# GLA scores in a fused transformer kernel: the diagonal moves from a level of its own into the finest level's matmuls

## The chip, the cores and the metric

The kernel runs on one core of a Trainium2 chip. A core has TensorE (matmuls, from SBUF into PSUM; PE in the profile, its weight loads PEld), VectorE (DVE), ScalarE (ACT), GpSimd (POOL) and SyncE (SP, which issues the weight transfers here). The engines run side by side and wait for each other by semaphores. The metric is device time in microseconds of one execution of the whole program.

## The reference, cut to what matters

Two transformer blocks over 256 tokens of width 1024. The change touches only gated linear attention (GLA) in the second layer of the second block: 4 heads, keys of 128, values of 256, chunks of 64 tokens.

```python
def _gla_chunked(q, k, v, log_a):
    gc = jnp.cumsum(chunks(log_a), axis=3)
    def step(state, inp):
        qi, ki, vi, gi = inp
        g_end = gi[:, :, -1, :]
        o_inter = jnp.einsum('bhtd,bhdv->bhtv', qi * jnp.exp(gi), state)
        rel = gi[:, :, :, None, :] - gi[:, :, None, :, :]
        decay = jnp.exp(jnp.where(causal[:, :, None], rel, -jnp.inf))
        scores = jnp.einsum('bhtd,bhsd,bhtsd->bhts', qi, ki, decay)
        o_intra = jnp.einsum('bhts,bhsv->bhtv', scores, vi)
        state = jnp.exp(g_end)[..., None] * state + jnp.einsum(
            'bhsd,bhsv->bhdv', ki * jnp.exp(g_end[:, :, None, :] - gi), vi)
        return state, o_inter + o_intra
```

What has to come out is, for each head, a causal matrix of scores between queries t and keys s, each the sum over 128 key channels of q * k * exp(g_t - g_s), with g the running sum of log decays; then scores times values.

## The kernel before

**Layout.** Features lie on the 128 partitions and the 256 tokens along the free axis, in two tiles t of 128 tokens. `gla` holds 24 rows of 256: queries of the four heads are `gla[:, 0:4]`, keys `gla[:, 4:8]`, gates from 16 on. `D[0]` to `D[3]` are PSUM banks of 512 fp32 columns.

**Scores by levels.** exp(g_t - g_s) is split at a token m between s and t, into exp(g_t - g_m) on the query and exp(g_m - g_s) on the key. `LEVELS = (64, 32, 16, 8, 4, 2, 1)`: at level n the tokens fall into blocks of 2n, the right half of each block are queries, the left half keys, and m is the last token of the left half. So each pair s < t of one tile belongs to exactly one level, and the pairs s = t need no decay: they are level 0, the plain product of keys and queries, of which only the diagonal is kept. At level 1 (the seventh and finest) m is the key's own token, so keys are multiplied by exp(0). Scores between tile 0 and tile 1 come from an eighth pass, `scores_across`.

**Who does what, for level index i:**
- VectorE, `exponents(i)`: the differences of `gla_g` (running sums) into `gla_e` or `gla_z` by turns, in two instructions of 512 elements, one for each half.
- ScalarE, `decays(i)`: exp of all 1024 elements in place.
- VectorE, `decayed(i)`: keys and queries times these, in two instructions of 512 elements, into `gla_w[i % 2]`; then `level_ready`.
- TensorE, `gla_level(i)`: for each tile, four matmuls (one a head) of 128 keys against 64 queries, into a bank; level 0 has 128 queries.
- VectorE, `keep_level(i)`: for each tile one conditional copy from the bank into `gla_s` through `level_mask`, then `drained_dve`.

VectorE goes through `exponents(i + 1)`, `decayed(i)`, `keep_level(i - 1)` in the loop over i, and evicts weight chunks in between. The last `keep_level` and a copy of the scores across end in `gla_scores_done`, for which the output matmuls (`d<-gla_s,gla_v`) wait.

**Weight chunks.** All projections stream fp32 weights in chunks of 128 x 2048. ScalarE rounds a chunk to `w_hi` (L1121), VectorE subtracts for `w_lo` (L1625), and TensorE multiplies in three products (fp32r), waiting for `lo_done` at the start of each chunk. Chunks 4 to 7 of `gla_in` are the values, with 512 columns a matmul. TensorE takes these in the order chunk 4, level 0, chunk 5, level 1, chunk 6, levels 2 and 3, chunk 7, levels 4 and 5, chunk 8, levels 6 and 7, chunk 9 with `scores_across` in it at k = 6, then the output matmuls, their sums of squares, chunks 10 and 11, and the output projection. VectorE writes `w_lo` of chunk 5 right behind `decayed(1)` and ahead of `keep_level(0)`.

**Order.** Everything is written out by hand: each engine executes its own list in the order of the code, and a PSUM bank is taken with `acquire` once its last reader has counted up.

The lines of the profile: L592 every matmul, L1619 products (`mul`), L1625 subtractions (`sub`), L1622 additions, L1629 `fused`, L2353 the conditional copy in `keep_level`, L2392 the copy of the scores across, L1121 every ScalarE function.

Of the kernel before, what the change touches and what calls it, by code (L numbers as in the profile page):

```python
# [30 lines left out]
P = 128  # L31
T = 256
# [144 lines left out]
def program(nc, io, out):  # L177
    with ExitStack() as stack:
        place = {"at": (nc.sbuf_base + 31) // 32 * 32}

        def at(name, offset, shape, dtype=F32):
            return nc.alloc_sbuf_tensor_at(name, [P] + shape, dtype, offset=offset)
# [246 lines left out]
        def over(ap, n):  # L429

            return ap.unsqueeze(1).broadcast_to([P, n, ap.shape[-1]])
# [5 lines left out]
        def flat(ap):  # L437
            return ap.rearrange("p a t -> p (a t)")
# [16 lines left out]
        def right_halves(ap, n):  # L455

            return ap.rearrange("p (b x t) -> p b x t", x=2, t=n)[:, :, 1, :]
# [115 lines left out]
        def _(pe):  # L573
# [17 lines left out]
            def mm(out, lhsT, rhs, start=True, stop=True):  # L591
                return pe.matmul(out, lhsT, rhs, start=start, stop=stop, skip_group_check=True)  # L592
# [469 lines left out]

            def gla_level(i):

                if i == 0:
                    pe.wait_ge(evicted, FIRST_OUT["gla_in"] + 4)
                else:
                    pe.wait_ge(level_ready, count.next(level_ready))
                for t in range(TT):
                    b = (2 * i + t) % 4  # L1070
                    cols = slice(t * P, (t + 1) * P)
                    acquire(b)
                    for h in range(4):
                        if i == 0:
                            last = mm(D[b][:, h * P:(h + 1) * P], gla[:, 4 + h, cols], gla[:, h, cols])
                        else:
                            k = gla_w[i % 2][:, h, cols]
                            last = mm(D[b][:, h * P // 2:(h + 1) * P // 2], k, right_halves(k, LEVELS[i - 1]))
# [37 lines left out]
        def _(act):  # L1116
# [3 lines left out]
            def fn(out, in_, func=ACT.Copy, **kw):  # L1120
                return act.activation(out, in_, func, **kw)  # L1121
# [493 lines left out]
        def _(dve):  # L1615
            count = Counts(dve)

            def mul(out, a, b):
                return dve.tensor_tensor(out, a, b, ALU.mult)  # L1619
# [525 lines left out]
            def conv_ffn(layer, ple_moving):  # L2145
# [117 lines left out]
                def half_finish(f):  # L2263

                    dve.wait_ge(act_done, count.next(act_done))
                    m, tile = ple_mul[:, 1, f, :], x[:, 6 + f, :]
                    mul(m, ple_sig[:, 1, f, :], D[3][:, f * T:(f + 1) * T]).then_inc(drained_dve, count.one(drained_dve))
                    dve.wait_ge(drained_dve, count.sent[drained_dve])
                    add(tile, tile, m).then_inc(x_gated, count.one(x_gated))

                half_evict(0)
# [16 lines left out]

            def gla_evict(j, split=True):
                if j < 2:  # L2290
                    fused(gla[:, 2 * j:2 * j + 2, :], bank_of("gla_in", j, j % U), float(P) ** -0.5, over(rstd[:], 2),
                                    ALU.mult, ALU.mult).then_inc(evicted, count.one(evicted))
# [39 lines left out]
            def decayed(i):  # L2332

                e = (gla_e, gla_z)[i % 2]
                dve.wait_ge(expo_done, count.next(expo_done))
                level = LEVELS[i - 1] if i <= len(LEVELS) else P
                to, ev = blocks(gla_w[i % 2], level), blocks(e, level)
                q, k = (flat(gla[:, f:f + 4, :]).rearrange("p (b h t) -> p b h t", h=2, t=level) for f in (0, 4))
                mul(to[:, :, 0, :], k[:, :, 0, :], ev[:, :, 0, :]).then_inc(dve_own, count.one(dve_own))
                mul(to[:, :, 1, :], q[:, :, 1, :], ev[:, :, 1, :]).then_inc(level_ready, count.one(level_ready))  # L2340

            def keep_level(i):

                dve.wait_ge(drained_dve, count.sent[drained_dve])
                for t in range(TT):
                    dve.wait_ge(full_dve, count.next(full_dve))
                    to, keep, found = gla_s[:, t, :, :], over(level_mask[:, i, :], 4), as_tiles(D[(2 * i + t) % 4][:], P)
                    if i > 0:
                        n = LEVELS[i - 1]
                        to = to.rearrange("p h (b x t) -> p h b x t", x=2, t=n)[:, :, :, 1, :]  # L2350
                        keep = right_halves(level_mask[:, i, :], n).unsqueeze(1).broadcast_to([P, 4, P // (2 * n), n])
                        found = D[(2 * i + t) % 4][:, 0:2 * P].rearrange("p (h b t) -> p h b t", h=4, t=n)
                    dve.copy_predicated(to, keep, found).then_inc(drained_dve, count.one(drained_dve))  # L2353

            ahead("gla_in", 0, 0)
            token_norm()
# [19 lines left out]
            for i in range(1, len(LEVELS) + 1):  # L2376
                if i > 1:
                    dve.wait_ge(level_ready, count.sent[level_ready])
                if i < len(LEVELS):
                    exponents(i + 1)  # L2380
                decayed(i)
                if i == len(LEVELS):
                    exponents(i + 1)
                if i == 1:
                    ahead("gla_in", 3, 0)
                keep_level(i - 1)
                if i in evictions:
                    gla_evict(evictions[i])
            decayed(len(LEVELS) + 1)
# [180 lines left out]
```

## Time and profile before

| | us |
|---|---|
| median of 3 runs | 1025.76 (1025.67 to 1025.93) |
| profiled execution | 1025.8, its span 1023.9 |
| TensorE busy (matmul / weight load) | 1016.1 / 989.9 |
| VectorE busy | 805.7 |
| ScalarE busy | 642.9 |
| mean granted clock of TensorE | 0.999 of 2.4 GHz |

The span is what lies between the first and the last instruction; the rest of the execution's time lies around it. The profile shows an fp32 matmul as two passes, each with a weight load of its own. A pass in the records lasts from its issue to the end of its drain, some 0.28 us for 128 columns, while the next one starts earlier; so what a pass costs is read from the distance of starts, not from its duration.

### The profile page before, as it was taken

To read this page: it belongs to the slowest core of one execution; us is meant where nothing else is said; L and a number is where in the kernel's file an instruction comes from. 1 tells how busy PE (TensorE), PEld (TensorE's weight loads), DVE (VectorE), ACT (ScalarE), POOL (GpSimd) and SP (SyncE) were. 2 spreads that over 40 slices of the span, in tenths; PEclk is the share of its full clock that TensorE was granted. 3 is DMA by queue.
4 is the path that set the end of the run, shared out by engine and by line. 5 is a ranking of instruction groups with operands and counts; after the bars stand their busy time and mean duration, and the time that the engine had idled before them with its cause. 6 is when DMAs were issued, how large, how long until landed. Compare 5 with 4: busy or idle time off the path is not lost.

```text
span 1023.9 us, 21104 instructions
## 1 busy us (share of the span) xinstructions
PE 1016.1 (99%) x8522; PEld 989.9 (97%) x8522; DVE 805.7 (79%) x960; ACT 642.9 (63%) x866; POOL 3.0 (0%) x9
## 2 busy tenths in 40 slices
PE   8999999999999999999999999999999999999998
PEld 7888999899999999999999999999899999999998
DVE  6879976586666756999887777798998888777787
ACT  7666665566455347676785756676546678657573
POOL 0000000000000000000000000010000000000000
PEclk9999999999999999999999999999999999999999
DMA  9942463355555564634655555564433565555541
GB/s 345 279 171 83 165 229 143 124 194 189 192 181 201 199 218 160 196 133 171 220 198 186 213 194 180 173 218 149 157 109 121 180 233 205 183 198 202 192 152 68
DMA packets 30543, 186.99 MB, mean 183 GB/s; under 512 B 3730, under 2 KB 6515, under 8 KB 8852
## 3 DMA queue, kind: packets, MB, share of 16 engines
q1 hardware_dynamic: 29908, 185.09, 51.6%
q8 instruction: 45, 0.74, 0.3%
q10 hardware_dynamic: 576, 1.05, 0.3%
q14 instruction: 14, 0.11, 0.0%
HBM read 183.99 MB, written 1.34 MB: 181 GB/s over the span
## 4 chain that ended last, share of the span: by engine, by line
PE 95%; DVE 3%; DMA 1%; ACT 0%; issue 0%; SPq 0%; DVEq 0%
PE g L592 62%; PE d L592 32%; DVE w_lo L1625 1%; PE d L595 1%; DMA raw<-weights 1%; DVE gla_w L1619 0%; DVE gla_o L1619 0%; DVE go_both L1629 0%; PE g L595 0%; DVE gla_s L2353 0%; DVE ho_both L1625 0%; DVE newton L1619 0%; DVE newton L1629 0%; ACT ho_both L1121 0%; DVE gla_v L1763 0%
## 5 line engine op out<-in xcount | busy, mean ns | idle before, releaser
L1625 DVE TENSOR_TENSOR w_lo<-raw,w_hi 128x2048 fp32r<-128x2048 f32 (+1 forms) x175 | 389.0, 2226 | 88.6 <-ACT w_hi L1121 88.3
L1121 ACT ACTIVATE w_hi<-raw 128x2048 fp32r<-128x2048 f32 (+1 forms) x174 | 326.2, 1878 | 142.4 <-PE g L592 84.4
L592 PE MATMUL g<-f_both,w_hi 128*128 128x256 f32 x1408 | 240.8, 275 | 0.0
L592 PEld LDWEIGHTS g<-f_both,w_hi 128*128 128x128 f32 x1408 | 212.0, 188 | 0.1
L592 PE MATMUL g<-f_both,w_lo 128*128 128x256 f32 x704 | 193.6, 275 | 0.0
L592 PE MATMUL d<-hid_lo,w_hi 128*128 (+1 forms) x528 | 145.2, 275 | 0.0
L592 PE MATMUL d<-hid_hi,w_lo 128*128 (+1 forms) x528 | 145.2, 275 | 0.0
L592 PE MATMUL d<-hid_hi,w_hi 128*128 (+1 forms) x528 | 145.2, 275 | 0.0
L592 PEld LDWEIGHTS g<-f_both,w_lo 128*128 128x128 f32 x704 | 132.2, 188 | 0.0
L592 PE MATMUL g<-x_both,w_hi 128*128 128x256 f32 x704 | 120.0, 275 | 0.0
L592 PEld LDWEIGHTS g<-x_both,w_hi 128*128 128x128 f32 x704 | 106.0, 188 | 0.1
L592 PEld LDWEIGHTS d<-hid_hi,w_hi 128*128 128x128 f32 x528 | 99.1, 188 | 0.0
L592 PEld LDWEIGHTS d<-hid_lo,w_hi 128*128 128x128 f32 x528 | 99.1, 188 | 0.0
L592 PEld LDWEIGHTS d<-hid_hi,w_lo 128*128 128x128 f32 x528 | 99.1, 188 | 0.0
L592 PE MATMUL g<-x_both,w_lo 128*128 128x256 f32 x352 | 96.8, 275 | 0.0
L592 PEld LDWEIGHTS g<-x_both,w_lo 128*128 128x128 f32 x352 | 66.1, 188 | 0.0
L592 PE MATMUL g<-hy_both,w_hi 128*128 128x256 f32 x288 | 50.4, 279 | 0.0
L1121 ACT ACTIVATE conv_out<-conv_in,par 128x256 f32<-128x256 f32 x88 | 47.5, 588 | 1.0 <-DVE conv_in L1619 1.0
L592 PE MATMUL g<-in_both,w_hi 128*128 128x256 f32 x256 | 45.1, 279 | 1.6 <-DVE w_lo L1625 1.6
L592 PE MATMUL g<-gla_both,w_hi 128*128 128x256 f32 x256 | 45.3, 280 | 0.0
L592 PE MATMUL g<-p_both,w_hi 128*128 128x256 f32 x256 | 44.2, 277 | 0.0
L592 PEld LDWEIGHTS g<-hy_both,w_hi 128*128 128x128 f32 x288 | 43.6, 188 | 0.6 <-DVE w_lo L1625 0.3
(363 smaller groups left out, 1964.0 us busy)
## 6 DMA issues: line engine op xcount, KB each, us to landing
raw<-weights SPq DMA_DIRECT2D x168, 1024.0 KB, 4.8
bias_tab<-bias_dram SPq DMA_DIRECT2D x8, 192.0 KB, 7.4
x<-x_t ACTq DMA_DIRECT2D x4, 256.0 KB, 5.5
raw<-weights SPq DMA_DIRECT2D x4, 256.0 KB, 6.6
raw<-weights SPq DMA_DIRECT2D x2, 512.0 KB, 7.4
mem_t<-mem_t SPq DMA_DIRECT2D x1, 1024.0 KB, 9.3
out<-x SPq DMA_DIRECT2D x3, 256.0 KB, 2.2
hy_swap<-hy_qk SPq DMA_DIRECT2D x4, 128.0 KB, 6.0
```

Source lines behind the costliest of these rows:

```text
L592: return pe.matmul(out, lhsT, rhs, start=start, stop=stop, skip_group_check=True)
L595: return pe.transpose(out, src, ident[0:n, 0:n])
L1121: return act.activation(out, in_, func, **kw)
L1625: return dve.tensor_tensor(out, a, b, ALU.subtract)
```

## The change

The diagonal no longer has a matmul of its own. The queries are evicted into a new tile `gla_q`, for each head and tile a row of 192 = 128 queries as they are and 64 places for the finest level's decayed queries. At the finest level the keys need no decay, so only `exponents` and `decayed` for the queries are left (one instruction each, instead of two), ScalarE's exp takes 512 elements instead of 1024, and TensorE multiplies the plain keys with the row of 192. Two heads then fill a bank with 384 columns, so the level takes four banks instead of two. `keep_level` of that level makes, for each tile and pair of heads, two conditional copies: the diagonal of 2 x 128, then the finest scores of 2 x 64, and the second waits for the first since both write `gla_s`. All other levels read the queries from `gla_q`. One increment of a semaphore in the gate of the embedding moves from `drained_dve` to `dve_own`.

```diff
+        gla_q = at("gla_q", TR, [4, TT, 3 * P // 2])
+        FINEST = 3 * P // 2
+        def finest_bank(t, pair):
+            return (2 * len(LEVELS) + 2 * t + pair) % 4
...
             def gla_level(i):
-                if i == 0:
-                    pe.wait_ge(evicted, FIRST_OUT["gla_in"] + 4)
-                else:
-                    pe.wait_ge(level_ready, count.next(level_ready))
+                pe.wait_ge(level_ready, count.next(level_ready))
                 for t in range(TT):
+                    cols = slice(t * P, (t + 1) * P)
+                    if i == len(LEVELS):
+                        for pair in range(2):
+                            b = finest_bank(t, pair)
+                            acquire(b)
+                            for f in range(2):
+                                h = 2 * pair + f
+                                last = mm(D[b][:, f * FINEST:(f + 1) * FINEST], gla[:, 4 + h, cols], gla_q[:, h, t, :])
+                            fill(b, last, full_dve, drained_dve)
+                        continue
...
             gla_chunk(4)
-            gla_level(0)
             gla_chunk(5)
...
+                if i == len(LEVELS):
+                    e = e[:, 1::2]
                 fn(e, e, ACT.Exp, scale=1.0 / 16.0).then_inc(expo_done, 1)
...
+                    if level == 1:
+                        sub(to[:, :, 1, :], s[:, :, 1, :], middle).then_inc(decay_done, 1)
+                        return
...
+                if i == len(LEVELS):
+                    to = gla_q[:, :, :, P:FINEST].rearrange("p h t c -> p (h t) c")
+                    mul(to, queries[:, :, :, 0], factors[:, :, :, 0]).then_inc(level_ready, count.one(level_ready))
+                    return
...
+                    for pair in range(2):
+                        dve.wait_ge(full_dve, count.next(full_dve))
+                        to = gla_s[:, t, 2 * pair:2 * pair + 2, :]
+                        found = D[finest_bank(t, pair)][:, 0:2 * FINEST].rearrange("p (h c) -> p h c", h=2)
+                        dve.copy_predicated(to, over(level_mask[:, 0, :], 2), found[:, :, 0:P]).then_inc(dve_own, count.one(dve_own))
+                        dve.wait_ge(dve_own, count.sent[dve_own])
+                        dve.copy_predicated(right_of(to), keep.broadcast_to([P, 2, P // 2, 1]), found[:, :, P:FINEST].unsqueeze(3)).then_inc(drained_dve, count.one(drained_dve))
...
-                keep_level(i - 1)
+                if i > 1:
+                    keep_level(i - 1)
```

TensorE at the border of chunk 4 and chunk 5 (`d<-gla` is level 0), before:

```order
L592 MATMUL g<-w_hi,gla_both 128x512
L592 MATMUL d<-gla 128x128 [waits lr_ready,evicted]
L592 MATMUL d<-gla 128x128 x3
L592 MATMUL d<-gla 128x128 [waits drained_dve]
L592 MATMUL d<-gla 128x128 x3
L592 MATMUL g<-w_hi,gla_both 128x512 [waits lo_done]
```

and now (lines are 7 further down in the new file):

```order
L599 MATMUL g<-w_lo,gla_both 128x512
L599 MATMUL g<-w_hi,gla_both 128x512
L599 MATMUL g<-w_hi,gla_both 128x512 [waits lo_done]
L599 MATMUL g<-w_lo,gla_both 128x512
L599 MATMUL g<-w_hi,gla_both 128x512 x2
```

The last matmul of chunk 4 is followed directly by the first of chunk 5, which waits for its low weights.

VectorE behind the decayed tiles of level index 1 (`gla_w_167`), before:

```order
L1619 TENSOR_TENSOR gla_w_167<-gla,gla_z 128x8x64 [waits expo_done]
L1619 TENSOR_TENSOR gla_w_167<-gla,gla_z 128x8x64
L1625 TENSOR_TENSOR w_lo<-raw,w_hi 128x2048 [waits hi_done]
L2353 COPY_PREDICATED gla_s<-level_mask,d 128x512 [waits full_dve,drained_dve]
L2353 COPY_PREDICATED gla_s<-level_mask,d 128x512 [waits full_dve]
L1625 TENSOR_TENSOR w_lo<-raw,w_hi 128x2048 [waits hi_done]
L1625 TENSOR_TENSOR gla_z<-gla_g 128x32x16 [waits level_ready]
```

and now:

```order
L1630 TENSOR_TENSOR gla_w_167<-gla,gla_z 128x8x64 [waits expo_done]
L1630 TENSOR_TENSOR gla_w_167<-gla_q,gla_z 128x8x64
L1636 TENSOR_TENSOR w_lo<-raw,w_hi 128x2048 [waits hi_done] x2
L1636 TENSOR_TENSOR gla_z<-gla_g 128x32x16 [waits level_ready]
L1636 TENSOR_TENSOR gla_z<-gla_g 128x32x16
```

Chunk 5's subtraction stands where it stood; the two conditional copies behind it are gone and chunk 6's subtraction has moved up to it.

VectorE at the end of the levels, from the products for the scores across (`gla_w_166`), before:

```order
L1619 TENSOR_TENSOR gla_w_166<-gla,gla_e 128x4x128 [waits expo_done]
L1619 TENSOR_TENSOR gla_w_166<-gla,gla_e 128x4x128
L2353 COPY_PREDICATED gla_s<-level_mask,d 128x256 [waits full_dve,drained_dve]
L2353 COPY_PREDICATED gla_s<-level_mask,d 128x256 [waits full_dve]
L2392 COPY gla_s<-d 128x512 [waits full_dve]
```

and now:

```order
L1630 TENSOR_TENSOR gla_w_166<-gla,gla_e 128x4x128 [waits expo_done]
L1630 TENSOR_TENSOR gla_w_166<-gla_q,gla_e 128x4x128
L2391 COPY_PREDICATED gla_s<-level_mask,d 128x256 [waits full_dve,drained_dve]
L2393 COPY_PREDICATED gla_s<-level_mask,d 128x128 [waits dve_own]
L2391 COPY_PREDICATED gla_s<-level_mask,d 128x256 [waits full_dve]
L2393 COPY_PREDICATED gla_s<-level_mask,d 128x128 [waits dve_own]
...
L2433 COPY gla_s<-d 128x512 [waits full_dve]
```

The pair of conditional copies stands there four times in the new order, ahead of the same copy of the scores across.

## Rows read from the trace of the kernel before

**Rows 1.** The page's first part: busy us, share of the span, instructions.

```profile
PE 1016.1 (99%) x8522; PEld 989.9 (97%) x8522; DVE 805.7 (79%) x960; ACT 642.9 (63%) x866; POOL 3.0 (0%) x9
```

**Rows 2.** Timeline of weight loads that waited: start, us, instruction, [idle before <-releaser].

```profile
728.07 0.19 PEld L592 LDWEIGHTS g<-w_hi,gla_both 128*128 128x128 f32 x1 [0.23 <-DVE w_lo L1625]
...
767.24 0.97 PEld L592 LDWEIGHTS d<-gla_w 128*128 128x128 f32 x8 [0.31 <-DVE gla_w L1619]
777.65 0.73 PEld L592 LDWEIGHTS d<-gla_w,const 128*128 128x128 f32 x4 [0.28 <-ACT gla_w L1121]
...
793.89 0.30 PEld L592 LDWEIGHTS d<-go_both,w_hi 128*128 128x128 f32 x2 [0.33 <-DVE go_both L1629]
```

**Rows 3.** The same view: level 0, its weight loads and its matmuls.

```profile
725.86 1.98 PEld L592 LDWEIGHTS d<-gla 128*128 128x128 f32 x16
...
726.09 1.95 PE L592 MATMUL d<-gla 128*128 128x128 f32 x16
```

**Rows 4.** Timeline of VectorE around chunk 5's low weights and the first merges.

```profile
714.99 0.69 DVE L1619 TENSOR_TENSOR gla<-g,rstd 128x512 f32<-128x512 f32 x1 [0.96 <-PE g L592]
...
725.73 2.28 DVE L1625 TENSOR_TENSOR w_lo<-raw,w_hi 128x2048 fp32r<-128x2048 f32 x1
727.93 1.34 DVE L2353 COPY_PREDICATED gla_s<-level_mask,d 128x512 f32<-128x512 uint8 x2
...
734.80 0.45 DVE L2353 COPY_PREDICATED gla_s<-level_mask,d 128x256 f32<-128x256 uint8 x1 [0.95 <-PE d L592]
```

**Rows 5.** Timeline of weight loads: levels 6 and 7, and chunk 9 behind them.

```profile
759.16 3.66 PEld L592 LDWEIGHTS d<-gla_w 128*128 128x128 f32 x32
762.74 0.30 PEld L592 LDWEIGHTS g<-gla_both,w_hi 128*128 128x128 f32 x2
```

**Rows 6.** Timeline of matmuls: plain fp32 with 256 columns, in two runs of 8 passes.

```profile
775.02 1.89 PE L592 MATMUL d<-sq,const 128*128 128x256 f32 x8
776.75 2.04 PE L592 MATMUL d<-gla_w,const 128*128 128x256 f32 x8
```

**Rows 7.** Timeline of VectorE from the exponents of level 7 to chunk 9's eviction.

```profile
756.01 1.29 DVE L1625 TENSOR_TENSOR gla_z<-gla_g 128x512 f32<-128x512 f32 x2
757.21 1.29 DVE L1619 TENSOR_TENSOR gla_w<-gla,gla_e 128x512 f32<-128x512 f32 x2
...
759.08 1.28 DVE L1619 TENSOR_TENSOR gla_w<-gla,gla_z 128x512 f32<-128x512 f32 x2
760.28 0.75 DVE L1625 TENSOR_TENSOR gla_e<-gla_g 128x256 f32<-128x256 f32 x2
...
765.90 1.28 DVE L1619 TENSOR_TENSOR gla_w<-gla,gla_e 128x512 f32<-128x512 f32 x2
767.11 1.29 DVE L2353 COPY_PREDICATED gla_s<-level_mask,d 128x256 f32<-128x256 uint8 x2
768.44 0.69 DVE L2392 COPY gla_s<-d 128x512 f32<-128x512 f32 x1
769.86 0.69 DVE L1619 TENSOR_TENSOR gla<-g,rstd 128x512 f32<-128x512 f32 x1 [0.73 <-PE g L592]
```

**Rows 8.** Timeline of weight loads: rest of chunk 9, then the output matmuls.

```profile
768.13 0.30 PEld L592 LDWEIGHTS g<-gla_both,w_hi 128*128 128x128 f32 x2
...
769.55 0.30 PEld L592 LDWEIGHTS d<-gla_s,gla_v 128*128 128x128 f32 x2
```

**Rows 9.** Timeline of VectorE: an instruction that reads the result of the one ahead.

```profile
779.62 0.69 DVE L1629 SCALAR_TENSOR_TENSOR newton<-mean_sq,rough 128x512 f32<-128x512 f32 x1
780.35 0.69 DVE L1619 TENSOR_TENSOR newton<-newton,rough 128x512 f32<-128x512 f32 x1
```

**Rows 10.** A stretch by engine (PEclk is the granted clock), and its longest wait.

```profile
5.00:10.00 5.00, 3.40 (x22) 2.75 (x22) 3.92 (x9) 4.19 (x10) 0.00 (x0) 1.00 1.02 368
...
7.13 0.30 PEld L592 LDWEIGHTS g<-in_both,w_hi 128*128 128x128 f32 x2 [1.62 <-DVE w_lo L1625]
```

More of the change, by code:

```diff
@@ L1063, in gla_level @@
             def gla_level(i):
-                if i == 0:
-                    pe.wait_ge(evicted, FIRST_OUT["gla_in"] + 4)
-                else:
-                    pe.wait_ge(level_ready, count.next(level_ready))
+                pe.wait_ge(level_ready, count.next(level_ready))
                 for t in range(TT):
+                    cols = slice(t * P, (t + 1) * P)
[8 more added lines that the diff above has]
+                        continue
                     b = (2 * i + t) % 4
-                    cols = slice(t * P, (t + 1) * P)
                     acquire(b)
                     for h in range(4):
[L1074 to L1078, printed above, removed]
+                        k = gla_w[i % 2][:, h, cols]
+                        last = mm(D[b][:, h * P // 2:(h + 1) * P // 2], k, right_halves(k, LEVELS[i - 1]))
                     fill(b, last, full_dve, drained_dve)
             gla_chunk(4)
-            gla_level(0)
             gla_chunk(5)
@@ L2266, in half_finish @@
                     m, tile = ple_mul[:, 1, f, :], x[:, 6 + f, :]
-                    mul(m, ple_sig[:, 1, f, :], D[3][:, f * T:(f + 1) * T]).then_inc(drained_dve, count.one(drained_dve))
-                    dve.wait_ge(drained_dve, count.sent[drained_dve])
+                    own = (dve_own, drained_dve)[f]
+                    mul(m, ple_sig[:, 1, f, :], D[3][:, f * T:(f + 1) * T]).then_inc(own, count.one(own))
+                    dve.wait_ge(own, count.sent[own])
                     add(tile, tile, m).then_inc(x_gated, count.one(x_gated))
@@ L2290, in gla_evict @@
                 if j < 2:
-                    fused(gla[:, 2 * j:2 * j + 2, :], bank_of("gla_in", j, j % U), float(P) ** -0.5, over(rstd[:], 2),
-                                    ALU.mult, ALU.mult).then_inc(evicted, count.one(evicted))
+                    bank = bank_of("gla_in", j, j % U).rearrange("p f (t c) -> p f t c", c=P)
+                    scale = rstd[:].rearrange("p (t c) -> p t c", c=P).unsqueeze(1).broadcast_to([P, 2, TT, P])
+                    fused(gla_q[:, 2 * j:2 * j + 2, :, 0:P], bank, float(P) ** -0.5, scale, ALU.mult, ALU.mult).then_inc(evicted, count.one(evicted))
                     if j == 1:
@@ L2335, in decayed @@
                 dve.wait_ge(expo_done, count.next(expo_done))
-                level = LEVELS[i - 1] if i <= len(LEVELS) else P
-                to, ev = blocks(gla_w[i % 2], level), blocks(e, level)
-                q, k = (flat(gla[:, f:f + 4, :]).rearrange("p (b h t) -> p b h t", h=2, t=level) for f in (0, 4))
+                if i > len(LEVELS):
+                    mul(gla_w[0][:, :, 0:P], gla[:, 4:8, 0:P], e[:, :, 0:P]).then_inc(dve_own, count.one(dve_own))
+                    mul(gla_w[0][:, :, P:2 * P], gla_q[:, :, 1, 0:P], e[:, :, P:2 * P]).then_inc(level_ready, count.one(level_ready))
+                    return
@@ new lines, in decayed, with in_tiles @@
+                level = LEVELS[i - 1]
+                def in_tiles(ap):
+                    return ap.rearrange("p a (b x n) -> p a b x n", x=2, n=level)
+                queries = in_tiles(gla_q[:, :, :, 0:P].rearrange("p h t c -> p (h t) c"))[:, :, :, 1, :]
+                factors = in_tiles(flat(e).rearrange("p (a c) -> p a c", c=P))[:, :, :, 1, :]
+                if i == len(LEVELS):
+                    to = gla_q[:, :, :, P:FINEST].rearrange("p h t c -> p (h t) c")
+                    mul(to, queries[:, :, :, 0], factors[:, :, :, 0]).then_inc(level_ready, count.one(level_ready))
+                    return
@@ L2339, in decayed @@
+                to, ev, k = blocks(gla_w[i % 2], level), blocks(e, level), blocks(gla[:, 4:8, :], level)
+                right = in_tiles(flat(gla_w[i % 2]).rearrange("p (a c) -> p a c", c=P))[:, :, :, 1, :]
                 mul(to[:, :, 0, :], k[:, :, 0, :], ev[:, :, 0, :]).then_inc(dve_own, count.one(dve_own))
-                mul(to[:, :, 1, :], q[:, :, 1, :], ev[:, :, 1, :]).then_inc(level_ready, count.one(level_ready))
+                mul(right, queries, factors).then_inc(level_ready, count.one(level_ready))
@@ L2342, in keep_level, with right_of @@
             def keep_level(i):
                 dve.wait_ge(drained_dve, count.sent[drained_dve])
+                n = LEVELS[i - 1]
+                keep = right_halves(level_mask[:, i, :], n).unsqueeze(1)
+                def right_of(scores):
+                    return scores.rearrange("p h (b x t) -> p h b x t", x=2, t=n)[:, :, :, 1, :]
                 for t in range(TT):
-                    dve.wait_ge(full_dve, count.next(full_dve))
-                    to, keep, found = gla_s[:, t, :, :], over(level_mask[:, i, :], 4), as_tiles(D[(2 * i + t) % 4][:], P)
@@ L2348, in keep_level @@
[L2348 to L2351, printed above, removed]
-                        found = D[(2 * i + t) % 4][:, 0:2 * P].rearrange("p (h b t) -> p h b t", h=4, t=n)
-                    dve.copy_predicated(to, keep, found).then_inc(drained_dve, count.one(drained_dve))
+                    if i < len(LEVELS):
+                        dve.wait_ge(full_dve, count.next(full_dve))
+                        found = D[(2 * i + t) % 4][:, 0:2 * P].rearrange("p (h b t) -> p h b t", h=4, t=n)
+                        dve.copy_predicated(right_of(gla_s[:, t, :, :]), keep.broadcast_to([P, 4, P // (2 * n), n]), found).then_inc(drained_dve, count.one(drained_dve))
+                        continue
@@ new lines, in keep_level @@
+                    for pair in range(2):
+                        dve.wait_ge(full_dve, count.next(full_dve))
+                        to = gla_s[:, t, 2 * pair:2 * pair + 2, :]
[3 more added lines that the diff above has]
+                        dve.copy_predicated(right_of(to), keep.broadcast_to([P, 2, P // 2, 1]), found[:, :, P:FINEST].unsqueeze(3)).then_inc(drained_dve, count.one(drained_dve))
```

## The prediction

> **What bounds the kernel now.** I read the busy shares of the page first, then every wait of TensorE's weight loads over the whole span, then the stretch from 724 to 794 us engine by engine, because only there the change moves anything. The page says that TensorE is busy for all but about 8 us of the span [rows 1]; so an edit counts by what it does to the row of TensorE's instructions, and time that another engine wins counts only where TensorE waits for it. From the GLA levels to the end such waits are four: 0.23 us for the low part of chunk 5's weights, 0.31 us for the decayed tiles of the scores across chunks, 0.28 us for a square of ScalarE and 0.33 us at the output projection [rows 2]. VectorE is nearly full in the same stretch, so it is the second engine to follow; ScalarE waits for VectorE there.
>
> **Level 0 goes.** Its 8 matmuls are 16 passes (each fp32 matmul shows as two). Their weight loads begin at 725.86 [rows 3] and the next weight load, chunk 5's first, stands at 728.07 with 0.23 idle before it [rows 2]. So they take 2.21 - 0.23 = 1.98 us of TensorE, and I ask what comes next in the row: chunk 5, which waits for the whole low part of its weights. VectorE writes that part from 725.73 to 728.01 [rows 4], and TensorE starts 0.06 later. Nothing ahead of that subtraction on VectorE is removed: the diff takes away only the merge of level 0, which stands behind it. So TensorE arrives 1.98 us earlier and waits 2.2 us instead of 0.23. Gained: **0**. The two evictions of the queries now write pieces of 128 in rows of 192; their element count is the same, and I cost that at nothing: VectorE waits 0.96 us for TensorE a little later, at 714.99, which hides any slowness below that [rows 4].
>
> **VectorE without the merge of level 0.** Two conditional copies of 512 elements, 1.34 us [rows 4], go. The two subtractions behind them move forward, and then VectorE meets the merge of level 1, for which it already waits 0.95 us [rows 4]. That wait grows to about 2.2 us and the merge starts where it did. Gained: 0. The earlier low part of chunk 6 also lets SyncE issue one weight transfer 1.2 us earlier; nobody waits for it.
>
> **Level 7 on TensorE.** Before, levels 6 and 7 are 32 passes of 64 columns from 759.16 to 762.74, 0.112 us each [rows 5]. A pass of 128 columns is no dearer: 16 of them cover 1.95 us with the last one's 0.28 in it, again 0.11 [rows 3]. A pass of 256 columns in plain fp32 takes (776.75 - 775.02) / 8 = 0.216 us [rows 6], twice that of 128. So moving data is what a wide pass costs, and the smaller value is a floor. No fp32 pass of 192 columns with full weights is in the trace: the bounds are the floor, 0.112, and the pass of 256, 0.216. I take the latter by its columns, 0.216 x 192 / 256 = 0.162, since above the floor time should go with columns. 16 passes then cost 16 x 0.050 = **+0.80 us** (bounds 0 and +1.66). Banks do not hold it up: the four banks are those of levels 5 and 6, and VectorE's merge of level 6 ends, as worked out below, earlier than now.
>
> Here the Trainium skill says otherwise ("TensorE: Matmul & The Clock Gate", Back-to-back issue gap and LDWEIGHTS): a warm matmul streams one column per cycle, N / 2.4 + 2.5 ns, and a load of 128 weights takes 128 / 1.2. By that 192 columns would take 82 ns, hide under a load of 107 ns, and level 7 would cost nothing more. The trace disagrees for plain fp32 with its 0.216 us for 256 columns, which is two cycles a column, so I go by the row.
>
> **The wait of 0.31 us ahead of the scores across.** VectorE's row from 756 us: the exponents of level 7 lose one of two subtractions, (757.21 - 756.01) / 2 = 0.60 us; the decayed tiles of level 7 lose one of two products, (760.28 - 759.08) / 2 = 0.60 us [rows 7]. ScalarE's exponential for this level handles half the elements and is ready earlier. So the products for the scores across start 1.20 us earlier than 765.90 [rows 7], and the 0.31 us of TensorE [rows 2] vanish. TensorE reaches that place 0.80 later than its old arrival, so against the old start the shift is 0.80 - 0.31 = **+0.49 us**. All that follows on TensorE, the 12 remaining passes of chunk 9 and then the output matmuls at 769.55 [rows 8], moves to 770.04.
>
> **The last merge, which grows.** The output matmuls also wait for VectorE: merge of level 7, then the copy of the scores across, now done at 768.44 + 0.69 = 769.13 [rows 7], so 0.42 us to spare. The merge was two conditional copies, 1.29 us [rows 7]. It becomes eight: for each tile and pair of heads 256 diagonal elements in a row, and then 128 at every second place, each of these four waiting for the one before it. The trace has no such copy of 128, so I build it. A copy of 256 in a row takes 0.45 alone, one of 512 takes (1.34 + 0.09) / 2 = 0.715 [rows 4]; 0.09 is the overlap of neighbours (1.29 against a next start 1.20 later) [rows 7]. So 256 elements cost 0.265 and the fixed part is 0.185. At every second place 256 elements take (1.29 + 0.09) / 2 = 0.69, so 0.505 for the elements; 128 of them take 0.25 + 0.185 = 0.44. A dependent instruction starts 0.04 after its source ends: 780.35 against 779.62 + 0.69 [rows 9]. One pair is (0.45 - 0.09) + 0.04 + 0.44 = 0.84, four are 3.4 us, **+2.1 us** on VectorE. With the 1.20 won before, the copy ends 0.9 later, at 770.03. TensorE wants it at 770.04. So the added merging is just hidden, with no margin. Bounds of the 128-element copy: 0.32 at the rate of elements in a row (0.5 less in all, hidden), 0.69 if it costs as much as 256 do (1.0 more, and TensorE waits for all of it).
>
> **What follows is carried along.** The squares, for which TensorE waits 0.28 us on ScalarE, start from the eviction of chunk 9 at 769.86 [rows 2, 7], which follows TensorE's chunk 9 and so moves by the same 0.5; the wait of 0.33 us at 793.89 [rows 2] ends a chain of VectorE that starts at TensorE's sums. Both keep their size. From 793.89 there is no wait of TensorE left to absorb a shift.
>
> **Sum.** 0 (level 0) + 0.80 - 0.31 + 0 = +0.5 us on the profiled execution's own 1025.8 us (span 1023.9 and 1.9 around it), which is 0.04 above the median of 1025.76. Forecast **1026.3 us**: the change takes TensorE 1.2 us of work off and the end still comes half a microsecond later.
>
> **Rivals.**
> - *Forecast*, shift 0.2 to 0.9 us: 60%.
> - *VectorE's last merge decides.* The 128-element copies cost 0.5 to 0.7 each and their waits add up: scores ready up to 1.0 later than TensorE wants them, 1026.6 to 1027.4. For it: no margin in the sum, and four new waits in a row on one engine. Against: half the elements. 20%.
> - *Cheap wide pass.* Level 7 at 0.112 a pass, as the page's rule would have it. TensorE then arrives 0.31 early, at 769.24, and waits for VectorE's 770.03, so it is again +0.5; only with the copies at 0.32 too the scores are ready at 769.5 and the shift is 0: 1025.8. 11%.
> - *The saving is kept.* If chunk 5 starts up to 1.98 us earlier after all (VectorE's row ahead of it shorter than I see), later merges find their banks earlier too, since VectorE waits for TensorE at level 1: -1.98 + 0.5 = -1.5, 1024.3. Against: the release 0.06 after the subtraction's end. 4%.
> - *Slower: the clock.* TensorE is now idle for about 2.2 us at 726. If it is granted 1.2 GHz afterwards, passes take double until it rises again; a stretch of 3.2 us at the lower level loses 1.6 us and, on top of 0.5, passes the bound of slower; 6 us would give 1029.3. Against: after 1.62 us of idle at 7.13 the granted clock of that stretch is 1.00 [rows 10]. No idle as long as 2.2 us is in the trace. The Trainium skill's rule that the chip's activity monitor halves the array's clock after idleness ("TensorE: Matmul & The Clock Gate", The HAM clock gate) is what speaks against this change; at 1.62 us the trace does not show it. 5%.
>
> **How the numbers follow.** A measurement of this kernel can tell about 0.2%, 2.05 us, from no change. Forecast, merge rival, cheap pass and kept saving all lie within it: same 93%. Slower than 1027.8 needs the clock: with both upper bounds, a pass of 0.216 and a copy of 0.69, TensorE comes 1.35 and VectorE's scores 1.5 later, and only the later of the two counts: 5%. Faster than 1023.7 needs more than the whole of level 0: 2%. The range for 8 in 10 goes from 1025.5, a little below the zero shift, to 1027.4, the upper bound of the merge; outside lie the kept saving, the clock, and some of each edge.
>
> **What would show it.** In the profile after: a wait of about 2.2 us of TensorE for the low weights near 728.07, at an unchanged start; 16 passes of level 7 0.16 apart; no wait ahead of the scores across, which start near 767.7; eight conditional copies over about 3.4 us; the output matmuls near 770.0 with at most a few tenths of wait. It would be wrong if chunk 5 starts much before 728, if the granted clock falls behind that wait, or if the copies of 128 run near 0.7.

## The result and the profile after

The changed kernel takes 1028.49 us (median of 10 runs, 1026.82 to 1029.04), the kernel before 1025.83 us beside it (10 runs, 1025.67 to 1026.00). The ratio is 1.0024, with a 95% interval of 1.0016 to 1.0032: 2.7 us slower where 0.5 was forecast, and outside the range of 1025.5 to 1027.4. The times of the changed kernel are in two groups with a gap between them: eight of 1028.2 to 1029.0 us, with a mean granted clock of 0.998, and two of 1026.8 and 1027.1 us, with 0.999 and 1.000. The profiled execution, 1029.04 us with a span of 1027.1, is of the first group. Both groups come back in every kernel below that has the same wait ahead of chunk 5, so they are taken here as the change's own.

TensorE is busy for 1016.8 us, 0.7 more than before [rows 1], though 16 passes are gone: what was saved came back as slower passes and waits, and the span is 3.2 us longer. The page's first part:

```profile
PE 1016.8 (99%) x8506; PEld 990.2 (96%) x8506; DVE 805.4 (78%) x962; ACT 642.8 (63%) x866; POOL 3.0 (0%) x9
```

The timeline of the changed kernel's weight loads that waited, to be held against [rows 2]:

```profile
728.47 0.19 PEld L599 LDWEIGHTS g<-w_hi,gla_both 128*128 128x128 f32 x1 [2.26 <-DVE w_lo L1636]
...
770.48 0.97 PEld L599 LDWEIGHTS d<-gla_w 128*128 128x128 f32 x8 [0.69 <-issue]
780.89 0.73 PEld L599 LDWEIGHTS d<-gla_w,const 128*128 128x128 f32 x4 [0.28 <-ACT gla_w L1130]
797.13 0.30 PEld L599 LDWEIGHTS d<-go_both,w_hi 128*128 128x128 f32 x2 [0.31 <-DVE go_both L1640]
```

The last two waits are the old ones. The first grew from 0.23 to 2.26 us, as forecast. The second should have gone and grew from 0.31 to 0.69. Read as differences to before, place by place, the delay is: +0.40 at chunk 5's start (728.47 against 728.07 [rows 2]), most of which arose in the first 10 us of the program, where the first chunks' transfers happened to land later and which the change does not touch (in a later profile of the same kernel, below, chunk 5 starts at 728.07 as before); +2.0 at level 6 (761.17 against 759.16 [rows 5]); +2.8 at the end of level 7; +3.2 at the scores across (770.48 against 767.24 [rows 2]), and it stays at that. So there are three steps: 1.6 us between 728 and 735, 0.8 at level 7, 0.5 at the scores across.

**The first step is TensorE's clock.** Stretches of the changed kernel: length, busy time (and instructions) of PE, PEld, DVE, ACT and POOL, then the granted clock, DMA share, GB/s:

```profile
726.00:728.00 2.00, 0.65 (x3) 0.19 (x1) 2.00 (x2) 2.00 (x2) 0.00 (x0) 1.00 0.00 0
728.00:729.00 1.00, 0.53 (x2) 0.43 (x3) 0.85 (x2) 0.53 (x1) 0.00 (x0) 0.83 0.00 0
729.00:730.00 1.00, 1.00 (x4) 0.82 (x3) 1.00 (x1) 0.00 (x0) 0.00 (x0) 0.50 0.92 131
...
731.00:732.00 1.00, 1.00 (x4) 0.76 (x3) 1.00 (x3) 0.00 (x0) 0.00 (x0) 0.50 1.07 451
732.00:733.00 1.00, 1.00 (x6) 0.83 (x5) 1.00 (x3) 0.91 (x1) 0.00 (x0) 0.96 0.94 352
```

0.50 is 1.2 GHz. TensorE has just been idle, it starts chunk 5, and from about 728.7 to 732.0 it gets half its clock. The fall does not come with the wait, during which the clock is still at 1.00, but 0.2 us after TensorE has started again. The matmuls of chunk 5 show it, first at the lower and then at the full clock:

```profile
728.92 0.63 PE L599 MATMUL g<-w_lo,gla_both 128*128 128x512 f32 x1
729.35 1.06 PE L599 MATMUL g<-w_hi,gla_both 128*128 128x512 f32 x2
730.20 0.63 PE L599 MATMUL g<-w_lo,gla_both 128*128 128x512 f32 x1
...
733.14 0.40 PE L599 MATMUL g<-w_lo,gla_both 128*128 128x512 f32 x1
733.38 0.63 PE L599 MATMUL g<-w_hi,gla_both 128*128 128x512 f32 x2
733.84 0.40 PE L599 MATMUL g<-w_lo,gla_both 128*128 128x512 f32 x1
```

Three passes take 730.20 - 728.92 = 1.28 us at 1.2 GHz and 733.84 - 733.14 = 0.70 at 2.4, so 3.4 us at the lower clock lose 3.4 x (1 - 0.70 / 1.28), an estimate of 1.5 us. What they did lose is read from the first weight load behind chunk 5, before and in the changed kernel:

```profile
733.46 1.98 PEld L592 LDWEIGHTS d<-gla_w 128*128 128x128 f32 x16
```

```profile
735.48 1.98 PEld L599 LDWEIGHTS d<-gla_w 128*128 128x128 f32 x16
```

Chunk 5 lasts 735.48 - 728.47 = 7.01 us instead of 733.46 - 728.07 = 5.39: 1.6 us. This is the rival of the clock in the prediction, almost to its number. The Trainium skill ("TensorE: Matmul & The Clock Gate", The HAM clock gate) has the rule that an array left idle is given 1.2 GHz until it has been busy again; by this stretch the trace agrees. In 25 of the 43 runs with this same wait (below) the clock did not fall.

**The second step is the wide pass.** Weight loads of level 7 and of what follows:

```profile
761.17 1.87 PEld L599 LDWEIGHTS d<-gla_w 128*128 128x128 f32 x16
762.97 2.58 PEld L599 LDWEIGHTS d<-gla_q,gla 128*128 128x128 f32 x16
765.52 0.35 PEld L599 LDWEIGHTS g<-gla_both,w_hi 128*128 128x128 f32 x2
```

16 passes of 192 columns take 765.52 - 762.97 = 2.55 us, 0.159 each; before, levels 6 and 7 with their 64 columns took 3.58 together [rows 5], so 1.79 each: +0.76.

**The third step is a bank.** VectorE in the same execution, from the first merge of the last level to the copy of the scores across:

```profile
767.90 0.44 DVE L2391 COPY_PREDICATED gla_s<-level_mask,d 128x256 f32<-128x256 uint8 x1
768.38 0.45 DVE L2393 COPY_PREDICATED gla_s<-level_mask,d 128x128 f32<-128x128 uint8 x1
768.63 0.49 DVE L2391 COPY_PREDICATED gla_s<-level_mask,d 128x256 f32<-128x256 uint8 x1
...
769.92 0.44 DVE L2393 COPY_PREDICATED gla_s<-level_mask,d 128x128 f32<-128x128 uint8 x1
...
770.68 0.44 DVE L2393 COPY_PREDICATED gla_s<-level_mask,d 128x128 f32<-128x128 uint8 x1
771.67 0.69 DVE L2433 COPY gla_s<-d 128x512 f32<-128x512 f32 x1 [0.56 <-PE d L599]
```

and the matmuls of the scores across:

```profile
770.51 1.13 PE L599 MATMUL d<-gla_w 128*128 128x128 f32 x8 [0.53 <-DVE gla_s L2393]
```

Before, level 7 used banks 2 and 3, and the scores across found bank 0 long drained. Now level 7 fills all four banks: tile 0 takes 2 and 3, tile 1 takes 0 and 1. Bank 0 holds the first pair of heads of tile 1, the third pair in the order of the merges, and the sixth copy, 769.92 + 0.44 = 770.36, frees it; TensorE starts 0.12 later. (The weight loads' own row names no releaser for the 0.69, only "issue"; the matmul's row names the merge, and the first experiment tests it.) And since VectorE's copy of the scores across waits for those matmuls in its turn, VectorE stands idle for 0.56 us.

### The profile page after: what moved, and what is told of

Read it like the earlier page. It is cut to its first block, busy times and chain, and to the rows that moved or that the text cites. A ratio compares the mean times of both kernels' runs of the same rounds, so it can differ in the third digit from the quotient of the medians.

```text
span 1027.1 us, 21072 instructions
## 1 busy us (share of the span) xinstructions
PE 1016.8 (99%) x8506; PEld 990.2 (96%) x8506; DVE 805.4 (78%) x962; ACT 642.8 (63%) x866; POOL 3.0 (0%) x9
## 4 chain that ended last, share of the span: by engine, by line
PE 93%; DVE 5%; DMA 1%; ACT 0%; issue 0%; SPq 0%; DVEq 0%
PE g L599 61%; PE d L599 31%; DVE w_lo L1636 1%; PE d L602 1%; DMA raw<-weights 1%; DVE gla_o L1630 0%; DVE gla_w L1630 0%; DVE go_both L1640 0%; PE g L602 0%; DVE gla_s L2385 0%; DVE gla_g L2409 0%; DVE gla L1630 0%; DVE ho_both L1636 0%; DVE gla_e L1636 0%; DVE newton L1630 0%
```

## The experiments

All times are medians with the kernel before beside them on the same chip. A run counts as one with a lowered clock where its mean granted clock is 0.998 or less; of such runs the kernel before had one (1026.80 us) in the 81 for which a clock was recorded. Three others of the 81 took 1027.5 to 1027.9 us at a mean clock of 0.999 or 1.000; no trace shows why. The fall itself is seen in two profiles, the changed kernel's and that of the longer gap; in all other runs it is inferred from the mean clock.

### The bank of the scores across

```diff
-                acquire(0)
+                acquire(2)
                 for h in range(4):
-                    last = mm(D[0][:, h * P:(h + 1) * P], gla_w[0][:, h, 0:P], gla_w[0][:, h, P:2 * P])
-                fill(0, last, full_dve, gla_scores_done)
+                    last = mm(D[2][:, h * P:(h + 1) * P], gla_w[0][:, h, 0:P], gla_w[0][:, h, P:2 * P])
+                fill(2, last, full_dve, gla_scores_done)
...
-            dve.tensor_copy(gla_s[:, 2, :, :], as_tiles(D[0][:], P)).then_inc(gla_scores_done, 1)
+            dve.tensor_copy(gla_s[:, 2, :, :], as_tiles(D[2][:], P)).then_inc(gla_scores_done, 1)
```

> The changed kernel, with the scores across written to bank D[2] instead of D[0]. Theory (two causes: TensorE's clock falls after the 2.26 us wait at chunk 5, worth 1.6 us, and the scores across wait for bank D[0] until the sixth of the eight merges, worth 0.77): the weight loads of the scores across follow the sixth k of chunk 9 without the 0.7 us gap, the output matmuls come 0.5 to 0.8 earlier, 1027.8 us. Rival (it is the longer merge on VectorE that ends last, and the bank only stands ahead of it): the copy of the scores across ends where it does now and the gap moves to the output matmuls, 1028.4 us, no gain.

Measured: 1026.63 us (11 runs) against 1025.88, ratio 1.0012 (1.0003 to 1.0021). The median falls between two groups again: seven runs of 1026.1 to 1026.7 us (mean 1026.4) and four of 1028.0 to 1028.2 (mean 1028.1) with the lowered clock. So the expected 1027.8 was wrong as a median, since I had reckoned the fall of the clock into every run; each group is 0.5 to 0.6 us below that of the changed kernel's first ten runs (1028.6 and 1026.9, the latter of two runs only). Weight loads, then VectorE, in this kernel's profile:

```profile
767.66 0.19 PEld L599 LDWEIGHTS g<-gla_both,w_lo 128*128 128x128 f32 x1
767.77 0.98 PEld L599 LDWEIGHTS d<-gla_w 128*128 128x128 f32 x8
...
770.09 0.53 PEld L599 LDWEIGHTS d<-gla_s,gla_v 128*128 128x128 f32 x4
```

```profile
768.76 0.45 DVE L2393 COPY_PREDICATED gla_s<-level_mask,d 128x128 f32<-128x128 uint8 x1
769.01 0.72 DVE L2433 COPY gla_s<-d 128x512 f32<-128x512 f32 x1
```

No wait is left ahead of the scores across, nor ahead of the output matmuls: VectorE is done at 769.73, TensorE comes at 770.09. Against the changed kernel's later profile, where chunk 5 starts at the same 728.07, the scores across start 768.55 - 767.77 = 0.78 us earlier. The rival, VectorE's longer merge, is out. This kernel, where the clock stays, is what the prediction described, and its 1026.4 us, 0.5 above before, are the forecast's 1026.3.

### Work in the gap

```diff
             gla_chunk(4)
+            pe.wait_ge(evicted, FIRST_OUT["gla_in"] + 4)
+            for t in range(TT):
+                cols = slice(t * P, (t + 1) * P)
+                acquire(t)
+                for h in range(4):
+                    mm(D[t][:, h * P:(h + 1) * P], gla[:, 4 + h, cols], gla[:, 4 + h, cols])
             gla_chunk(5)
```

> The changed kernel, with 8 matmuls of keys against keys (128 columns, results read by nobody) in the place of the old level 0, so that TensorE works through its wait for chunk 5. Theory (the idle time lowers the clock): chunk 5 still starts at its old time, granted clock 1.00 in every microsecond behind it, 24 passes in 5.6 us, and the run is 1.6 us faster than the changed kernel, 1026.9 to 1027.1 us, with the spread of the runs back to some tenths. Rival (the clock falls for another reason, such as the load of the matmuls of chunk 5 or of the level of 192 columns): it falls here too, 1028.5 us.

Measured: 1027.11 us, 11 runs of 1026.47 to 1027.30, none with a lowered clock; before 1025.88, ratio 1.0012 (1.0003 to 1.0021). The wait and the granted clock behind it:

```profile
728.28 0.19 PEld L599 LDWEIGHTS g<-w_hi,gla_both 128*128 128x128 f32 x1 [0.24 <-DVE w_lo L1642]
```

```profile
728.00:730.00 2.00, 1.95 (x11) 1.46 (x9) 1.85 (x2) 0.34 (x1) 0.00 (x0) 1.00 0.41 70
730.00:732.00 2.00, 2.00 (x10) 1.66 (x9) 2.00 (x4) 0.10 (x1) 0.00 (x0) 1.00 0.84 348
```

1.98 us of useless matmuls leave the kernel at 1027.1 us, where the changed kernel lies when its clock stays: 1.4 us below the median of its first ten runs, in which the clock mostly fell, and 0.2 below that of the eleven later ones, in which it mostly did not. Chunk 5 starts where it did. On the same chip the two other kernels with a wait of 2.26 us, the bank's and the one without level 0, had 7 lowered runs of 22, this one none of 11; by itself that could be chance (about 4 in 100 if the filling did nothing).

With half of these matmuls (two heads instead of four in the loop above):

> The changed kernel with 4 unread matmuls instead of 8 ahead of chunk 5, so that TensorE is idle for about 1.25 us there instead of 2.26. The start of chunk 5 is the same. If the clock falls only after the longer idle time, all executions lie at 1027.1 us like those with the gap filled; if the chance of a fall goes with the length, some 2 in 10 lie at 1028.6.

```profile
727.94 0.19 PEld L599 LDWEIGHTS g<-w_hi,gla_both 128*128 128x128 f32 x1 [1.12 <-DVE w_lo L1642]
```

Measured: 1027.09 us, 11 runs of 1026.81 to 1027.42, none with a lowered clock (before 1025.92, ratio 1.0011, 1.0002 to 1.0020). 1.12 us of idle did no harm in these. No kernel with the wait of 2.26 us ran on this chip beside it; the comparison is with series taken elsewhere. The two fillers together have 0 of 22, the kernels with the wait of 2.26 us 18 of 43 (below): it is the idle time that lets the clock fall.

### A longer gap

```diff
-                mul(to[:, :, 0, :], k[:, :, 0, :], ev[:, :, 0, :]).then_inc(dve_own, count.one(dve_own))
+                for n in range(3 if i == 1 else 1):
+                    if n:
+                        dve.wait_ge(dve_own, count.sent[dve_own])
+                    mul(to[:, :, 0, :], k[:, :, 0, :], ev[:, :, 0, :]).then_inc(dve_own, count.one(dve_own))
```

> The changed kernel with the keys' product of level index 1 made three times on VectorE, so that chunk 5's low weights come 1.45 us later and TensorE is idle for about 3.7 us. The delay itself costs 1.45: 1028.5 us with the clock kept. If the fall of the clock is a matter of idle length, as the theory has it, it falls in nearly all executions: 1030.1 us. If it is a matter of something else that the idle time only touches by chance, the share stays near the 4 in 10 of the other kernels with the wait of 2.26 us.

Measured: 1030.28 us, 5 runs; before 1025.92, ratio 1.0043 (1.0029 to 1.0057). Four of the five have a lowered clock (1030.27, 1030.28, 1031.20, 1031.26 us), one has not (1028.33). The wait, and the clock behind it:

```profile
729.83 0.19 PEld L599 LDWEIGHTS g<-w_hi,gla_both 128*128 128x128 f32 x1 [3.72 <-DVE w_lo L1636]
```

```profile
729.00:730.00 1.00, 0.17 (x1) 0.17 (x2) 1.00 (x2) 0.00 (x0) 0.00 (x0) 1.00 0.00 0
730.00:731.00 1.00, 1.00 (x4) 0.83 (x5) 1.00 (x1) 0.00 (x0) 0.00 (x0) 0.72 0.44 57
731.00:732.00 1.00, 1.00 (x3) 0.77 (x3) 1.00 (x2) 0.00 (x0) 0.00 (x0) 0.50 0.47 147
...
733.00:734.00 1.00, 1.00 (x4) 0.80 (x3) 1.00 (x3) 0.79 (x1) 0.00 (x0) 0.58 0.99 418
734.00:735.00 1.00, 1.00 (x6) 0.79 (x5) 0.39 (x1) 1.00 (x2) 0.00 (x0) 1.00 1.05 426
```

```profile
736.83 1.98 PEld L599 LDWEIGHTS d<-gla_w 128*128 128x128 f32 x16
```

The single run at 1028.33 is about the price of the delay alone (1028.5 expected). In the profiled run of 1030.27 the fall costs what it cost after 2.26 us: the clock is at 0.50 for about 3.4 us, and chunk 5 lasts 736.83 - 729.83 = 7.00 us instead of 5.39, 1.6 more. Here it falls only some 0.6 us after TensorE has started again. The two runs of 1031.2 and 1031.3 us, with a mean clock of 0.996, lose a microsecond more; no trace of them was kept, and why they do is open.

### The kernel before without level 0

```diff
             gla_chunk(4)
-            gla_level(0)
             gla_chunk(5)
...
-                keep_level(i - 1)
+                if i > 1:
+                    keep_level(i - 1)
```

> The kernel before, only without level 0: its 8 matmuls and its two conditional copies are left out, and nothing of the rest is changed, so the diagonal of the scores is missing. By the prediction on record this is worth 0 (wait instead of work): 1025.8 us. By the theory of the clock it is 1.6 us slower than before in most executions, 1027.4 us, and the granted clock reads 0.50 for some 3 us behind chunk 5's start. By a rival in which 2 us less work is a gain: 1024.1 us.

Measured: 1025.97 us (11 runs) against 1025.88, ratio 1.0003 (0.9994 to 1.0012). Eight runs of 1025.4 to 1026.3 us (mean 1025.8), three of 1027.0, 1027.6 and 1027.8 with the lowered clock. In its profile the clock happened to stay:

```profile
727.96 0.19 PEld L592 LDWEIGHTS g<-w_hi,gla_both 128*128 128x128 f32 x1 [2.26 <-DVE w_lo L1624]
```

```profile
729.00:730.00 1.00, 1.00 (x6) 0.82 (x5) 1.00 (x1) 0.00 (x0) 0.00 (x0) 1.00 0.76 156
```

Leaving out 1.98 us of TensorE's work is worth nothing at this place, which was the first step of the prediction, and costs 1.6 us in the executions where the clock falls (mean 1027.4 against 1025.8). The median expected from the clock, 1027.4, missed: only 3 of 11 fall.

### The changed kernel again

> The changed kernel again, nothing edited, for the share of executions in which the clock falls after the wait at chunk 5: 8 of the first 10, while the two other kernels with the same wait had 4 and 3 of 11. If the share belongs to the kernel, some 8 or 9 of 11 lie at 1028.5; if it belongs to the chip or to chance, 3 to 6 of 11, and the rest at 1027.1.

Measured: 1027.27 us (11 runs, 1026.85 to 1028.76) against 1025.87, ratio 1.0015 (1.0006 to 1.0024). Three of 11 have the lowered clock (1028.07, 1028.61, 1028.76), eight have not (1026.85 to 1027.66, mean 1027.1). So the same program has 8 of 10 one time and 3 of 11 another time (whether the chip or chance decides, two series can't tell); with the other two kernels that wait 2.26 us it is 18 of 43. The profile, with the same wait and the clock kept:

```profile
728.07 0.19 PEld L599 LDWEIGHTS g<-w_hi,gla_both 128*128 128x128 f32 x1 [2.26 <-DVE w_lo L1636]
...
768.55 0.97 PEld L599 LDWEIGHTS d<-gla_w 128*128 128x128 f32 x8 [0.71 <-issue]
```

```profile
729.00:730.00 1.00, 1.00 (x6) 0.81 (x5) 1.00 (x1) 0.00 (x0) 0.00 (x0) 1.00 0.95 131
```

From start to start of these two weight loads it is 768.55 - 728.07 = 40.48 us here and 770.48 - 728.47 = 42.01 in the profile with the lowered clock: 1.53 us. The groups of this kernel are 1.3 us apart in these eleven runs and 1.6 in the first ten, so the fall of the clock accounts for the difference.

### The low weights first

In the wait of 2.26 us lies the whole gain of the change, so I moved what it waits for. ScalarE rounds chunk 5 ahead of the first exponential, for which it stood idle 3.44 us, and VectorE subtracts ahead of the exponents and products of the first level, which TensorE needs only a chunk later.

```diff
-            decays(1)
             gla_ahead(3)
+            decays(1)
...
+                if i == 1:
+                    ahead("gla_in", 3, 0)
                 if i < len(LEVELS):
                     exponents(i + 1)
                 decayed(i)
                 if i == len(LEVELS):
                     exponents(i + 1)
-                if i == 1:
-                    ahead("gla_in", 3, 0)
```

> The changed kernel, with the low part of chunk 5's weights made earlier: ScalarE rounds chunk 5 ahead of the first exponential, and VectorE subtracts ahead of the exponents and products of level 1. Theory: chunk 5 follows chunk 4 without a wait, the 1.98 us of level 0 are kept and the clock stays at 1.00: 1.98 + 1.6 less than the changed kernel, 1025.0 us; what remains of it is a longer wait of the scores across for bank D[0], since VectorE has less idle time to give back, so up to 1025.6. Rival (VectorE is the bound of the whole stretch, so TensorE only waits elsewhere): 1026.9 us, as with the gap filled.

Measured: 1025.31 us (11 runs, 1024.94 to 1025.67, none with a lowered clock) against 1025.88, ratio 0.9994 (0.9985 to 1.0003). That is 1.8 us below the changed kernel with a kept clock: the level's 1.98 us, less what new waits take. VectorE, then the weight loads that waited:

```profile
723.41 2.29 DVE L1636 TENSOR_TENSOR w_lo<-raw,w_hi 128x2048 fp32r<-128x2048 f32 x1
...
729.83 2.29 DVE L1636 TENSOR_TENSOR w_lo<-raw,w_hi 128x2048 fp32r<-128x2048 f32 x1 [1.73 <-ACT w_hi L1130]
```

```profile
741.18 1.86 PEld L599 LDWEIGHTS d<-gla_w 128*128 128x128 f32 x16 [0.29 <-DVE gla_w L1630]
...
766.83 0.97 PEld L599 LDWEIGHTS d<-gla_w 128*128 128x128 f32 x8 [0.69 <-issue]
```

With the scores across in bank 2 as well:

> The changed kernel with both repairs: chunk 5's low weights made earlier, and the scores across in bank D[2]. If the two waits are separate costs, as the theory has it, both gains add up: 1025.3 - 0.75 = 1024.6 us, faster than the kernel before by 1.2. Rival (VectorE's row through the eight merges ends last once TensorE is 2 us earlier): the output matmuls wait for the copy of the scores across instead, 1025.0 to 1025.3 us.

Measured: 1024.61 us (11 runs, 1024.16 to 1025.21) against 1025.92, ratio 0.9988 (0.9979 to 0.9997). The gains add up.

And with ScalarE's rounding of chunk 6 moved ahead of the second exponential, so that VectorE's wait of 1.73 us goes:

```diff
+            gla_ahead(4)
             for i in range(1, len(LEVELS) + 1):
                 decays(i + 1)
-                for j in {1: (4,), 2: (5, 6), 3: (7,), 5: (8,), 7: (9,)}.get(i, ()):
+                for j in {2: (5, 6), 3: (7,), 5: (8,), 7: (9,)}.get(i, ()):
```

> As the kernel with both repairs, and ScalarE rounds chunk 6 right behind the first exponential, ahead of the second, for which it otherwise waits. With chunk 5's low part made earlier VectorE stood idle for 1.73 us for that rounding, and level 3 then came 0.29 us late for TensorE. Theory: that wait and the 0.29 go, 1024.3 us. Rival (TensorE's wait at level 3 is made up by slack ahead of the scores across): as both repairs alone, 1024.6 us.

Measured: 1024.40 us (11 runs, 1024.16 to 1024.61) against 1025.92, ratio 0.9985 (0.9976 to 0.9994). The wait at level 3 is gone from its profile. The further 0.2 us against the kernel with both repairs is inside the spread of either. This is the fastest version, 1.5 us below the kernel before. Its weight loads of the last levels and what follows, to be held against [rows 5, 8]:

```profile
759.05 2.58 PEld L599 LDWEIGHTS d<-gla_q,gla 128*128 128x128 f32 x16
765.79 0.98 PEld L599 LDWEIGHTS d<-gla_w 128*128 128x128 f32 x8
768.11 5.44 PEld L599 LDWEIGHTS d<-gla_s,gla_v 128*128 128x128 f32 x48
```

The scores across start 767.24 - 765.79 = 1.45 us and the output matmuls 769.55 - 768.11 = 1.44 us earlier than before, which is the gain.

The same move alone, in the kernel before:

> The kernel before, with its level 0, and chunk 5's low weights made earlier as in the repaired kernels. TensorE waited only 0.23 us for them, so no more than that can be won: 1025.7 us. With both repairs and the early rounding of chunk 6 the changed kernel takes 1024.4, so by the theory 1.3 us are the change's own, once nothing waits behind it. Rival: the earlier weights alone are worth most of it (1024.5 to 1025.0), and the shared matmul little.

Measured: 1025.56 us (11 runs, 1025.36 to 1025.77) against 1025.87, ratio 0.9995 (0.9986 to 1.0004): 0.3 us in the medians, about the 0.23 that TensorE waited there, and no more than the interval allows as nothing. So, by difference, some 1.2 of the 1.5 us of the fastest version are the shared matmul's own; the early rounding of chunk 6 was not tried in the kernel before.

## Why the prediction was wrong

- **Level 0 is worth nothing: right.** TensorE waits 2.26 us (2.2 forecast) and chunk 5 starts no earlier. The kernel before without level 0 shows it by itself, 1025.8 where the clock stays.
- **The clock: the step that failed.** The rival had its place, its mechanism and nearly its price (1.6 us for 3.2 us at the lower clock, a length that came from no row; 3.4 us at 0.50 and 1.6 us were measured), and got 5%. I had set against it the one row with a long idle, 1.62 us at the clock of 1.00 [rows 10], and added that no longer one was in the trace. A row for 1.62 us says nothing for 2.26: the clock fell in 18 of 43 runs there, in 8 of the 10 that made the result, in 4 of 5 after 3.72 us, and in none of 11 after 1.12. I had called the wait free because it took the place of work, and that is where 1.6 of the 2.7 us come from.
- **Level 7: right.** +0.76 measured, +0.80 forecast by columns. The page's rule that I had set beside it (one column a cycle, 82 ns for 192 columns; the Trainium skill, "TensorE: Matmul & The Clock Gate", Back-to-back issue gap) gives half of what plain fp32 takes here: 0.159 us a pass, 0.83 ns a column, against 0.84 for 256 columns [rows 6].
- **The wait ahead of the scores across goes: wrong, and the term that was missed.** I looked at the banks that level 7 has to wait for, not at the ones it now keeps. The products were ready earlier as forecast, but bank 0 was not drained; 0.31 of wait became 0.69. From the end of level 7 to the scores across TensorE lost 3.24 - 2.78 = 0.46 us, 0.38 of it in that wait, where -0.31 had been reckoned. So the shift at this place is +1.2 us with a kept clock (0.76 + 0.46) instead of +0.49. Moving one bank gave 0.5 to 0.6 us back.
- **The longer merge is just hidden: right.** Eight copies took 771.12 - 767.90 = 3.22 us (3.4 forecast), a copy of 128 elements 0.45 (0.44 forecast). With the other bank VectorE is done 0.36 us ahead of TensorE.
- **What follows is carried along: right.** The waits of 0.28 and 0.31 us kept their size.

So without the fall of the clock the changed kernel takes 1027.1 us, 1.2 above before: within the range, but more than double the forecast shift, and the bank accounts for the excess of some 0.7 us. With it, 1028.5. Which of the two is the median depends on how often it falls. What decides that share is open: the same kernel had 8 of 10 and 3 of 11, and no run here tests why.

## What to carry to other kernels

Before removing work from the engine that bounds a kernel, ask what it does next: where it then waits, nothing is won, and where the wait grows to the 2.26 us of this case, the clock may fall and the removal costs time. Move what it will wait for first (here two instructions, 2.3 and 1.9 us, that had slack on both sides), and then take the work out. When a step comes to use more buffers, look not only at whether it gets them but at who wanted one of them next.

## What the runs showed of the hardware

- After a wait of 2.26 us, counted between weight loads (1.82 between the matmuls' own rows), TensorE's granted clock fell to 0.50 for about 3.4 us in some executions of the same program and stayed at 1.00 in others. It fell not in the wait but 0.2 us after its end (0.6 us after a wait of 3.72), and cost 1.6 us. In the 66 runs of the six edited kernels whose wait there is at most 1.12 us it never fell, and in 81 of the kernel before one run was at 0.998.
- With unread matmuls in the wait the clock stayed in 11 of 11 runs, and in 11 of 11 with half of them, leaving 1.12 us idle.
- A plain fp32 pass costs its columns from somewhere between 128 (0.11 us, no more than 64 columns) and 192 (0.159 us) on.
- A conditional copy at every second place takes about twice the time per element of one in a row: 0.45 us for 128 elements, as for 256 in a row, of which an estimated 0.185 is fixed (from 0.45 us for 256 and 0.715 for 512 in a row).
